# Router matmul with the operands exchanged: the weights held, the tokens moved

## The reference

```python
h = x + merged @ w_out
hn = rmsnorm(h, g_ffn).reshape(B * L, D)
y = h + hier_moe(hn, w_group, b_group, w_router, b_router, w_gate, w_up, w_down)

# in hier_moe: top-1 group of 4, then top-2 of the 4 experts in it
gl = xf @ w_group + b_group            # (T, 4)
el = (xf @ w_router + b_router)        # (T, 16)
```

## Time and profile before

| | us |
|---|---|
| time, median of 3 runs | 2011.25 (2008.54 to 2011.75) |
| the profiled execution, its own time | 2014.13 |
| its span | 2012.4 |
| PE busy | 1877.3 (93%) |
| PE weight loads busy | 1609.9 (80%) |
| DVE busy | 974.0 (48%) |
| ACT busy | 773.4 (38%) |

### The profile page before, as it was taken

The page is one execution under the profiler, slowest core; times in us unless marked ns, Lnnn a source line. Parts: engine busy times, 40 slices in busy tenths (PEclk is TensorE's granted clock), DMA queues, the critical chain, the costliest instruction groups (busy, mean ns, idle before and its releaser), DMA issues. The chain is left out here.

```text
span 2012.4 us, 28492 instructions
## 1 busy us (share of the span) xinstructions
PE 1877.3 (93%) x10232; PEld 1609.9 (80%) x10233; DVE 974.0 (48%) x1929; ACT 773.4 (38%) x1442; POOL 280.8 (14%) x387
## 2 busy tenths in 40 slices
PE   7899999999999999999999937999999999999980
PEld 5899987788888788887888736888888888888870
DVE  5634343546444654445454334445565554646424
ACT  4332323333333333333333204444465444636423
POOL 2000000000201001000010022222222222222223
PEclk9799999999999999999999958999999999999995
DMA  6222233423236222342232517655567566556438
GB/s 220 88 83 84 84 128 119 138 86 102 85 126 209 84 85 96 135 138 93 84 105 87 198 47 230 186 183 184 177 215 257 152 230 188 183 182 228 130 56 343
DMA packets 153429, 293.12 MB, mean 146 GB/s; under 512 B 9341, under 2 KB 75901, under 8 KB 153354
## 3 DMA queue, kind: packets, MB, share of 16 engines
q1 hardware_dynamic: 135930, 232.13, 32.9%
q0 software_dynamic: 15072, 51.45, 10.4%
q10 hardware_dynamic: 2352, 8.52, 1.0%
HBM read 243.02 MB, written 49.07 MB: 145 GB/s over the span
## 5 line engine op out<-in xcount | busy, mean ns | idle before, releaser
L62 PE MATMUL bank<-xT_hi,wh 128*128 128x512 f32 (+1 forms) x960 | 341.0, 355 | 7.2 <-ACT S L745 5.4
L63 PE MATMUL bank<-xT_lo,wh 128*128 128x512 f32 (+1 forms) x960 | 340.4, 355 | 0.0
L64 PE MATMUL bank<-xT_hi,wl 128*128 128x512 f32 (+1 forms) x960 | 339.2, 353 | 0.0
L793 DVE TENSOR_TENSOR wl<-raw,wh 128x512 fp32r<-128x512 f32 x352 | 219.4, 686 | 202.5 <-ACT wh L596 202.4
L1665 PE MATMUL bank<-gu_hi,ex_hi 128*128 128x256 f32 (+1 forms) x960 | 311.6, 325 | 4.6 <-DVE gu_lo L1575 4.6
L1667 PE MATMUL bank<-gu_hi,ex_lo 128*128 128x256 f32 (+1 forms) x960 | 307.3, 320 | 0.0
L1666 PE MATMUL bank<-gu_lo,ex_hi 128*128 128x256 f32 (+1 forms) x960 | 307.3, 320 | 0.0
L596 ACT ACTIVATE wh<-raw 128x512 fp32r<-128x512 f32 x352 | 192.0, 619 | 85.1 <-PE bank L1216 54.7
L62 PEld LDWEIGHTS bank<-xT_hi,wh 128*128 128x128 f32 x960 | 182.3, 190 | 35.9 <-issue 9.7
L1665 PEld LDWEIGHTS bank<-gu_hi,ex_hi 128*128 128x128 f32 x960 | 183.5, 191 | 24.7 <-DVE gu_lo L1575 8.2
L64 PEld LDWEIGHTS bank<-xT_hi,wl 128*128 128x128 f32 x960 | 182.4, 190 | 25.3
(11 more groups left out here) (228 smaller groups left out, 3154.8 us busy)
## 6 DMA issues: line engine op xcount, KB each, us to landing
raw<-in_w_in SPq DMA_DIRECT2D x56, 1024.0 KB, 5.2
raw_gate_up<-in_w_gate SPq DMA_DIRECT2D x16, 2048.0 KB, 8.4
raw_gate_up<-in_w_up SPq DMA_DIRECT2D x16, 2048.0 KB, 13.5
raw_d<-in_w_down SPq DMA_DIRECT2D x16, 2048.0 KB, 12.8
raw<-in_w_out SPq DMA_DIRECT2D x16, 1024.0 KB, 6.3
raw<-in_w_up_pool SPq DMA_DIRECT2D x16, 512.0 KB, 3.5
raw<-in_w_up_gmlp SPq DMA_DIRECT2D x16, 512.0 KB, 4.5
h<-in_x_prompt SPq DMA_DIRECT2D x16, 512.0 KB, 5.0
```

The lines of the kernel that those rows point to most:

```text
L62: nc.tensor.matmul(out, lh, rh, start=(i == 0), stop=False)
L63: nc.tensor.matmul(out, lh, rl, start=False, stop=False)
L64: last = nc.tensor.matmul(out, ll, rh, start=False, stop=(i == n - 1))
L793: lo = lambda out, x, hi: tt(out, x, hi.bitcast(F32), ALU.subtract)
```

## The change

The router's product is turned round. `wr[:, k, :]`, 20 columns, is held in the array and the tokens of `hnT` are moved, so the logits come out with 20 partitions and the tokens along the row (`bankR[0:20, 0:r]`). VectorE adds the bias, now one value per partition, and writes `lgT` in SBUF (`add_bias`). TensorE transposes that back into other columns of the same bank, and VectorE copies the 20 logits per token to `lg` (`logits`). There are two new semaphores, `lt_full` and `lt_ok`.

The order is changed with it. TensorE does the transposes of tile t ahead of the router of tile t-1. ScalarE does the rounded copy to `vn` ahead of the two copies to `hnT`. VectorE adds the bias of tile t-1 at the end of the turn, and takes the logits of tile t-2 at its start. The bias is loaded as a column of 20 values instead of a broadcast to 128 partitions.

```diff
-        br = sb("br", [P, 20])
+        br = sb("br", [P, 1])
...
-                (br[:, 0:4], v["b_group"].broadcast_to([P, NG])),
-                (br[:, 4:20], v["b_router"].broadcast_to([P, NE])),
+                (br[0:4, :], v["b_group"].rearrange("a n -> n a")),
+                (br[4:20, :], v["b_router"].rearrange("a n -> n a")),
...
+                    if t < ph.nt2:
+                        r = ph.rows2[t]
+                        act.wait_ge(vf_ok, first2 + t + 1)
+                        nc.scalar.activation(vn[0][0:r, t, :], vf[0:r, :], ACT.Copy).then_inc(vn_hi, 1)
                     if t < ph.nt:
                         if t:
-                            act.wait_ge(lg_full, first + t)
+                            act.wait_ge(lt_full, first + t)
...
-                    if t < ph.nt2:
-                        r = ph.rows2[t]
-                        act.wait_ge(vf_ok, first2 + t + 1)
-                        nc.scalar.activation(vn[0][0:r, t, :], vf[0:r, :], ACT.Copy).then_inc(vn_hi, 1)
...
+            def add_bias(ph, t):
+                r = ph.rows[t]
+                dve.wait_ge(lt_full, ph.first + t + 1)
+                ts(lgT[0:20, 0:r], bankR[0:20, 0:r], br[0:20, 0:1], None, ALU.add).then_inc(lt_ok, 1)
+
             def logits(ph, t):
                 r = ph.rows[t]
                 dve.wait_ge(lg_full, ph.first + t + 1)
-                tt(lg[0:r, t, 0:4], bankR[0:r, 0:4], br[0:r, 0:4], ALU.add)
-                tt(lg[0:r, t, 8:24], bankR[0:r, 4:20], br[0:r, 4:20], ALU.add).then_inc(lg_ok, 1)
+                nc.vector.tensor_copy(lg[0:r, t, 0:4], bankR[0:r, P:P + 4])
+                nc.vector.tensor_copy(lg[0:r, t, 8:24], bankR[0:r, P + 4:P + 20]).then_inc(lg_ok, 1)
...
                 for t in range(max(ph.nt, ph.nt2)):
+                    if 1 < t < ph.nt:
+                        logits(ph, t - 2)
                     if t < ph.nt2:
                         norm_v(ph, t)
                     if t + 3 < ph.nt:
                         norm_h(ph, t + 3)
-                    if t < ph.nt and (t < ph.nt - 1 or not ph.next):
-                        logits(ph, t)
+                    if 0 < t < ph.nt:
+                        add_bias(ph, t - 1)
...
                 for k in range(KD):
-                    last = nc.tensor.matmul(bankR[0:r, 0:20], hnT[:, k, 0:r], wr[:, k, :], start=(k == 0),
+                    last = nc.tensor.matmul(bankR[0:20, 0:r], wr[:, k, :], hnT[:, k, 0:r], start=(k == 0),
                                             stop=(k == KD - 1))
-                last.then_inc(lg_full, 1)
+                last.then_inc(lt_full, 1)
+
+            def logits(ph, t):
+                r = ph.rows[t]
+                pe.wait_ge(lt_ok, ph.first + t + 1)
+                nc.tensor.transpose(bankR[0:r, P:P + 20], lgT[0:20, 0:r], ident[0:20, 0:20]).then_inc(lg_full, 1)
...
+                    if 1 < t < ph.nt:
+                        logits(ph, t - 2)
+                    if t < ph.nt:
+                        transpose_hn(ph, t)
                     if 0 < t < ph.nt:
                         router(ph, t - 1)
-                    if t < ph.nt:
-                        transpose_hn(ph, t)
                 if not ph.next:
+                    logits(ph, ph.nt - 2)
                     router(ph, ph.nt - 1)
+                    logits(ph, ph.nt - 1)
                     count(ph)
                     return
+                if ph.nt:
+                    logits(ph, ph.nt - 2)
                 chunk(ph, o + 2, 0, "a", 0, xT, every, ph.segs2)
```

More of the change, by code:

```diff
@@ L228, in phase_one @@
         hnT = sb("hnT", [P, KD, P])
-        sb("rest_of_pb", [P, h4_spare])
+        rest = sb("rest_of_pb", [P, h4_spare])
+        lgT = rest[:, 0:P]
         raw = [sb("raw0", [P, 8, 256]), sb("raw1", [P, 8, 256])]
@@ L314, in phase_one @@
         exps_in, exps_ok, spare_out = sem("exps_in"), sem("exps_ok"), sem("spare_out")
-        lg_full, lg_ok, mask_ok, cum_full, dest_ok, scattered = (sem(s) for s in (
-            "lg_full", "lg_ok", "mask_ok", "cum_full", "dest_ok", "scattered"))
+        lt_full, lt_ok, lg_full, lg_ok, mask_ok, cum_full, dest_ok, scattered = (sem(s) for s in (
+            "lt_full", "lt_ok", "lg_full", "lg_ok", "mask_ok", "cum_full", "dest_ok", "scattered"))
         hist_full, hist_ok, hist_out = sem("hist_full"), sem("hist_ok"), sem("hist_out")
@@ L1123, in body @@
                         norm_h(ph, t + 3)
-                    if t < ph.nt and (t < ph.nt - 1 or not ph.next):
-                        logits(ph, t)
+                    if 0 < t < ph.nt:
+                        add_bias(ph, t - 1)
                 if not ph.next:
+                    logits(ph, ph.nt - 2)
+                    add_bias(ph, ph.nt - 1)
+                    logits(ph, ph.nt - 1)
                     choose(ph)
@@ L1131, in body @@
                 if ph.nt:
+                    logits(ph, ph.nt - 2)
+                    add_bias(ph, ph.nt - 1)
+                pooled(ph, 0)
+                if ph.nt:
                     logits(ph, ph.nt - 1)
-                pooled(ph, 0)
                 pooled(ph, 1)
@@ L1233, in router @@
                 freed(pe, ph, "hn", t, 1)
-                if t:
+                if ph.first + t:
                     pe.wait_ge(lg_ok, ph.first + t)
                 for k in range(KD):
-                    last = nc.tensor.matmul(bankR[0:r, 0:20], hnT[:, k, 0:r], wr[:, k, :], start=(k == 0),
+                    last = nc.tensor.matmul(bankR[0:20, 0:r], wr[:, k, :], hnT[:, k, 0:r], start=(k == 0),
                                             stop=(k == KD - 1))
-                last.then_inc(lg_full, 1)
+                last.then_inc(lt_full, 1)
[3 more added lines that the diff above has]
+                nc.tensor.transpose(bankR[0:r, P:P + 20], lgT[0:20, 0:r], ident[0:20, 0:20]).then_inc(lg_full, 1)
             def count(ph):
```

## The result

The changed kernel takes 2016.8 us (median of 12 runs, 2011.7 to 2018.4), the kernel before 2011.3 us beside it on the same chip (12 runs, 2007.3 to 2012.3). The ratio is 1.0027, with a 95% interval of 1.0018 to 1.0035: slower by 5.5 us. The forecast was 2020.5 (2013 to 2029). The two profiled executions lie closer together than the medians: 2016.3 after and 2014.1 before, spans 2014.6 and 2012.4 us. The traced execution of the kernel before lies above all twelve runs beside it, at a mean granted clock of 0.958 where its runs in the experiments show 0.958 to 0.962, so the clock may give back more in this pair of traces than in the medians.

A forecast was written before the change was run, and what follows sets the result against it. PE (TensorE) was taken to bound the kernel, busy 93% of the span. Terms -0.8 + 1.4 + 6.0 + 2.6 + 0.4 + 1.1 - 1.5 = +9.2 us on a median of 2011.25 gave 2020.5, range 2013 to 2029.

The forecast's parts named there:

- Router's pitch: Router matmuls in groups 0 to 2: 109 ns each in place of 113, a gain of 0.8 us over 12 full tiles.
- one nor four cycles per column: Rivals on router passes: one cycle per moved column, 2010.3 us, chance 0.04; four cycles, 2053 us with group 3, chance 0.03.
- First tile: Loops of groups 0 to 2: PE waits for ScalarE's hnT copies, now behind the vn copy; +6.0 us together.
- Last tile: End of each loop: PE waits 1.3 us for VectorE's bias ahead of the last logits transpose; +2.6 us together.
- DVE: VectorE's two logits copies stand in the chain to chunk a3, where PE waits: +0.15 us per group, +0.4 in all.
- The transposes added: 17 transposes of logits, one per tile, 0.11 us each at full clock; 13 in groups 0 to 2, +1.4 us.
- Group 3, the tail: Group 3's loop, a chain without products at half clock: later first router, shorter router gap, added bias, transpose and drain; +1.1 us.
- the clock pays for it: Rival: wide routers keep the clock up in all loops and group 3; 2004.6 us, or 2013.6 without group 3; chance 0.08.
- the one on the count: Sign of being right: choose's first instruction comes about 1 us later against the start of group 3's loop.
- the sign of being wrong: In group 3's loop, a clock of 1.00 over 1152 to 1173 would show the forecast wrong.
- Clock in groups 0 to 2: 128 moved columns give back 3.3 us of half-clock stretches, less 1.8 for longer first-tile waits: net -1.5 us.
- the new waits let the clock fall: Rival: in groups 1 and 2 the new waits lower the clock, up to 10 us more, 2030 us; chance 0.12.

The follow-up runs named there:

- third experiment: The changed kernel, but on ScalarE tile 0's copies to hnT stand ahead of the vn copy: 2016.5 us, ratio 1.0029 to the kernel before.
- fourth experiment: The kernel before, its router moving its 20 columns six times over (120 columns, 100 outputs unread): 2003.2 us against 2010.8, ratio 0.9958.
- fifth experiment: The changed kernel with 8 unread products of 512 columns on PE ahead of tile 1's transposes in groups 0 to 2: 2014.3 us against 2010.2 before.
- sixth experiment: Operands exchanged, old orders, early bias, second bank, plus 12 unread products ahead of group 3's first transposes: 2004.2 us against 2010.2 for the kernel before.
- the two kernels at 2003 to 2004: Both have exchanged operands, old PE and ScalarE orders and a second bank: bias early on VectorE, 2002.9 us; bias on ScalarE, 2004.0 us.
- the bank alone: Transposed logits moved to another PSUM bank, against the changed kernel with old PE and ScalarE orders and ScalarE's bias: 2004.0 us, 2014.1 without.
- the exchange alone: The changed kernel with old PE and ScalarE orders, bias before VectorE's low half, transposed logits in another bank: 2002.9 us against 2010.8 for the kernel before.

## Why the prediction was right, and where it was not

The sign and the main mechanism were right: the waits that the new orders and the trip through VectorE bring cost more than the exchange gives. The sum was +9.2 us; the traces have 9.6 - 5.6 = +4.0 from group 0's loop to the count, the medians +5.5. That the number lies in the range is in part luck. Sorted by kind, the forecast and the traces are:

| | forecast | traces |
|---|---|---|
| waits of PE, groups 0 to 2 | +8.7 | +6.4 |
| clock, groups 0 to 2 | -1.5 | -3.4 |
| router, transposes and what stands between them, groups 0 to 2 | +0.9 | +6.6 (what is left of the 9.6) |
| group 3 | +1.1 | -5.6 |

The two last rows are wrong by +5.7 and -6.7 us, and cancel.

*Router's pitch: right, its term wrong.* The matmuls stand 109 ns apart, as forecast. Neither one nor four cycles per column came true. The Trainium skill, TensorE: Matmul & The Clock Gate, section Back-to-back issue gap, gives 134 cycles for 128 columns. That doesn't hold for these passes: 109 ns are 262 cycles of 2.4 GHz. But the gain of 0.8 us isn't there. Start to start, the router takes 1.85 us a tile against 1.71, 0.14 more and not 0.06 less.

*First tile: right in place, near in size.* 2.2, 3.0 and 2.0 us in groups 1, 0 and 2, for 1.7, 3.8 and 2.4. The third experiment adds what the prediction did not say: take this wait away alone, and much of it comes back as a wait for the bias.

*Last tile: right in place, near in size.* 1.0 us for 1.3. (The prediction's own terms, as they stand, give 4.1 + 0.25 - 2.75 = 1.6, and for group 0 1.3 + 0.5 - 0.8 = +1.0 and not +0.8; it didn't matter.) The bias takes 0.33 us and not the 0.16 that was assumed for it, but PE reaches the wait later too: from the transpose of logits at 638.53 over transposes and router to 641.57 (639.72 + 1.85) are 3.0 us, where the forecast had 2.75.

```profile
641.62 0.69 DVE L794 TENSOR_TENSOR mg_lo<-S,mg_hi 128x512 fp32r<-128x512 f32 x1 [0.70 <-ACT mg_hi L715]
642.23 0.33 DVE L888 TENSOR_SCALAR rest_of_pb<-bank,br 20x128 f32<-20x128 f32 x1
```

*"DVE": wrong in sign, small.* The waits ahead of the chunk that hangs on VectorE's copies didn't grow by 0.4 us, they shrank from 2.0 + 1.6 + 1.6 to 1.8 + 1.4 + 1.4.

*"The transposes added" and the router, taken as +0.6 us together: too small.* With the 0.3 us between the halves of the transposes they are the +0.9 of the table. All waits of PE at and behind the three loops (330 to 400, 600 to 665, 880 to 950) grow by 6.4 us (6.2 + 4.6 + 4.4 after, 4.5 + 2.0 + 2.3 before), and the clock gives 3.4 back, (17.0 - 10.3)/2 by the lengths of the half-clock stretches. With +9.6 measured, 6.6 are left for everything else. The steady turn shows them: +0.62 where the sum had +0.05. Of these 0.16 are the transpose of logits; the other 0.46 lie at the changes from one shape of matmul to the next, where the loads are exposed. A row of the kernel before had this sign. Its router with 32 columns held begins at 374.45, and its loads begin with it; I read the row for the pitch alone.

```profile
374.45 0.58 PEld L1237 LDWEIGHTS bank<-wr,hnT 128*32 128x32 f32 x16 [0.37 <-issue]
```

*"Group 3, the tail. No products stand here, the clock is at half": the step that failed.* Forecast +1.1 us, measured -5.6. The start of the chain was read rightly (the first router comes 2.0 us later against the loop's start, for 1.8), but the clock was taken as given, at half throughout, though the change alters just the matmuls of this loop. The fourth experiment shows the cause without anything else of the change: moving more columns brings the clock back there after 3.4 us. The rival "the clock pays for it" names this very place, and its condition came true: of the 18.1 us from the first transposes to the last transpose of logits (1158.61 to 1176.69), 11.9 are at full clock. It had only 0.08. Its price came out too large: for group 3 it stands 9 us below the forecast's +1.1, so at -7.9, and -5.6 were measured; for groups 0 to 2 it had -8.4 and -3.4 were measured. Of the signs, the one on the count came out the other way (5.6 us earlier against group 3's loop, and not 1 later), and the sign of being wrong, a clock of 1.00 over the loop of group 3, came in part.

*Clock in groups 0 to 2.* Net -1.5 forecast, -3.4 measured. The stretches of the rival "the new waits let the clock fall" came in groups 1 and 2, 3.4 us long where its price took 6.7; the fifth experiment ties them to the waits. That narrow routers let the clock fall was right as far as the fourth experiment goes, but the stretches at 387.5 there and at 386.4 in the sixth stand behind full products and a wait. In group 0 one stretch of 3.4 us stands where two of 6.8 were.

So the change is two things. The exchange, freed of queueing, is worth -7.9 us, in the main by the granted clock: at full clock its turn is longer than before (5.83 us against 5.40); the new orders, the late bias and the shared bank take 13.9 back. Each of the two kernels at 2003 to 2004 undoes several of these at once, and of the bank alone (2014.1 to 2004.0) the price is shown only with the bias on ScalarE. What an early bias in the one bank would give was not run. The clock is read from one traced execution of each kernel, and single stretches at half clock can come and go with no edit near them, as the sixth experiment shows; the medians carry the ratios, the traces the account of where the time went.

## What to carry to other kernels

When a result makes an extra trip between engines (PE, VectorE, PE), place each leg in its engine's queue, and see which engines a shared bank ties together; one leg put right alone can merely move the wait. Ask of every change of matmul shape what it does to the clock, first in the stretch where the clock is already at half, and try the shape alone, as the kernel with 120 moved columns does, before the data flow is rebuilt for it. And measure a loop by its steady turn, start to start, and not by the pitch of its matmuls: what changes hands between unlike matmuls is not in the pitch.

## What the runs showed of the hardware

- Moving 120 in place of 20 columns in float32 passes, at the same weight loads and nearly the same pace (a turn of 5.44 for 5.40 us), made the kernel 7.6 us faster through the granted clock.
- In the changed kernel, after a wait of 2 to 3 us, passes with 20 held columns ran at half clock for 3.4 us, in all three groups. With the wait filled by unread products all three stretches were gone; with 112 held and the wait still there, two of three. Whether there the columns held, the shorter wait (1.7 for 2.2 us in group 1; but 2.3 for 2.0 in group 2) or the moment of the wait did it is open.
- A wait of PE between products of 512 columns in group 0 was followed by 3.4 us at half clock in two kernels (2.0 us, stretch at 387.5; 1.8 us, stretch at 386.4), and the same wait by none in the kernel before (2.0 us) and in the exchange alone (1.8 us). So a wait's length alone doesn't say whether the clock falls.
- Float32 passes of 128 moved columns start 109 ns apart at full clock, whether 20 or 112 columns are held, and 213 ns apart at half. Passes of 20 and of 120 moved columns with 128 held start 112 ns apart.
- From and to the router of 20 held columns the weight load isn't put ahead of the running matmul; each stage of the turn is 0.12 to 0.20 us longer than before. With 112 held the turn fell from 6.02 to 5.71 us behind the transposes of `hn`, and only from 5.83 to 5.76 where the transpose of logits stands ahead of the router. Why is open.
